# One decoder layer on one core: an opening with fewer waits, and a third expert pair returned to tokens by one-hot products

## The chip, the cores and the metric

The kernel runs on one core of a Trainium2 chip. The metric is the device time of one execution in microseconds. TensorE multiplies matrices into the eight banks of PSUM; VectorE (DVE), ScalarE (ACT) and GpSimd (POOL) work elementwise; SyncE (SP) and the others issue DMAs, which 16 DMA engines carry out.

## The reference

One layer of a decoder on x (512 tokens, 1024 channels), in float32:

```python
mod = silu(c) @ w_ada + b_ada                      # six vectors: shift, scale, gate, twice
h = rmsnorm(x, norm1) * (1 + sc1) + sh1
z = h @ w_in                                       # q, k, v, pooling input, two gates
merged = sigmoid(ga) * attention_branch + sigmoid(gp) * pooling_branch
x = x + g1 * (merged @ w_out)
h = rmsnorm(x, norm2) * (1 + sc2) + sh2
# router: best of 4 groups, then the best 2 of its 8 experts; weights e_w
for each of 32 experts e:
    hid = silu(h @ w1[e]) * (h @ w3[e]) * combine[:, e]      # 256 hidden channels
    out = out + hid @ w2[e]
x = x + g2 * out
```

w_ada is 24 MB, w_in 16 MB, and each expert has 3 MB of weights (w1, w3 and w2 of 1 MB each), 96 MB in all.

## The kernel before, in words

**Opening.** SP loads c, then the chunks of w_ada, x and w_in one behind the other, on one queue. TensorE forms the first two vectors of `mod` as rows (`ada_rows`) and turns them into columns (`ada_columns`), and transposes the normed x (`x_transposes`). Before the transposes it waits in program order for eight small vectors (`small_loaded`), since one small product (`vecs`, line 778) stands there. `keep_warm` is a helper that issues products nobody reads. The first unit of the w_in projection (line 638) then needs the columns of `mod`, hT, which ScalarE and VectorE make from them, and the first chunk of w_in.

**Middle.** 32 units of 128 output columns or rows with the attention, pooling and merging beside them, then `project`, the residual, the second norm and the router. SP starts on expert weights as arena space comes free.

**Routing.** VectorE copies the router's logits out of PSUM (line 1544) and picks experts; TensorE ranks the tokens; `one_hot` writes a matrix of tokens by slots for the pairs of experts in three groups (pairs 0 and 1, 2 and 3, 4 to 15). A pair is two experts of 64 slots each. `slot_sums` (line 887) multiplies these by token numbers (`tokb`, N = 2) and by the second choice (`oh2b`, N = 2) in products of their own; `indices` makes from them the rows to gather and to scatter. GpSimd gathers 128 rows of a pair from memory (line 1940).

**Pairs.** Step q runs `gate_up(q)` (w1 and w3, line 930), `gather_transposes(q + 1)`, `down(q - 1)` (w2, line 966), with tanh and copies on ScalarE and `modulate_gathered`, `hidden`, `drain_y` on VectorE, each in the order written. Six slots of weights form a ring, so three pairs are loaded ahead. SP waits until a pair's slots are free and issues the loads of the pair that follows; for experts 6 and 7 it does so by halves, the first half after four of the eight k of pair 0 (`ab_half`, lines 526 and on). The third group of slot sums stands inside `gate_up(1)`.

**End.** The results of pairs 0 to 13 go to `y_scratch` in memory by an indirect DMA (line 1945). When these have landed, SP loads them back by token, in four loads of 1 MB (`rows_of`, line 578), and VectorE adds the two rows of each token, weighted (`add_stored`, line 1690). Pairs 14 and 15 (`LAST = 2`) stay on the chip: `drain_last` (line 1673) weights them, ScalarE and VectorE split them into two parts (`y_high` line 1236, `y_low` line 1683), and TensorE multiplies by a one-hot matrix of slots and tokens (`spread`, line 983), two products for each of eight tiles and each pair. `down(15)` waits until `drain_last(0)` has emptied its PSUM banks. At last VectorE adds each of the eight tiles (line 1783) and SP stores it.

## Time and profile before

| | us |
|---|---|
| median of three runs | 651.97 (650.91 to 656.72) |
| the profiled execution's own time | 651.78 |
| its span, first to last instruction | 650.0 |
| TensorE busy | 579.4 (89%) |
| VectorE busy | 298.2 (46%) |
| ScalarE busy | 154.5 (24%) |
| DMA | 173.82 MB, mean 267 GB/s |

Busy time is a sum over stages with different limits, so it does not say which engine sets the time of a stage. The page's row by slices does: it has the DMA rate in each fortieth of the span. Mean granted clock of TensorE is 0.962 of full.

### The profile page before, as it was taken

To read this page: it belongs to the slowest core of one execution; us is meant where nothing else is said; L and a number is where in the kernel's file an instruction comes from. 1 tells how busy PE (TensorE), PEld (TensorE's weight loads), DVE (VectorE), ACT (ScalarE), POOL (GpSimd) and SP (SyncE) were. 2 spreads that over 40 slices of the span, in tenths; PEclk is the share of its full clock that TensorE was granted. 3 is DMA by queue.
4 is the path that set the end of the run, shared out by engine and by line. 5 is a ranking of instruction groups with operands and counts; after the bars stand their busy time and mean duration, and the time that the engine had idled before them with its cause. 6 is when DMAs were issued, how large, how long until landed. Compare 5 with 4: busy or idle time off the path is not lost.

```text
span 650.0 us, 7287 instructions
## 1 busy us (share of the span) xinstructions
PE 579.4 (89%) x2780; PEld 334.3 (51%) x2780; DVE 298.2 (46%) x580; ACT 154.5 (24%) x336; POOL 96.0 (15%) x144
## 2 busy tenths in 40 slices
PE   2699899999999999999999998999977888797891
PEld 0454577777766676764588844433322333232341
DVE  0227977455746565129624486323222222245258
ACT  3016013244433434333202302112111111111110
POOL 3022233059400000000000011111111111101000
PEclk9689899999999999999999989999998889898997
DMA  8994763403490606051457595899999999999873
GB/s 312 398 355 175 270 248 140 152 1 130 163 354 22 238 1 259 2 204 55 177 234 300 183 421 163 319 417 420 419 420 421 418 422 420 420 419 420 373 301 131
DMA packets 42073, 173.82 MB, mean 267 GB/s; under 512 B 6333, under 2 KB 6397, under 8 KB 29749
## 3 DMA queue, kind: packets, MB, share of 16 engines
q1 hardware_dynamic: 34704, 159.40, 61.9%
q0 software_dynamic: 5744, 12.84, 5.4%
q10 hardware_dynamic: 1588, 1.10, 0.5%
q8 instruction: 23, 0.38, 0.2%
q14 instruction: 14, 0.11, 0.0%
HBM read 165.36 MB, written 15.74 MB: 279 GB/s over the span
## 4 chain that ended last, share of the span: by engine, by line
PE 67%; DMA 10%; issue 8%; DVE 6%; SPq 4%; POOL 3%; ACTq 1%; ACT 0%; DVEq 0%; POOLq 0%
PE bank L930 15%; PE bank L966 7%; PE bank L649 5%; PE bank L651 5%; PE bank L650 5%; PE bank L739 4%; DMA late<-in_w_dram 4%; SPq L518 3%; POOL ss L1909 3%; DMA late<-in_w_in_dram 3%; DMA qkg<-in_k_norm_dram 2%; PE bank L831 2%; PE bank L833 2%; PE bank L832 2%; PE bank L913 2%
## 5 line engine op out<-in xcount | busy, mean ns | idle before, releaser
L930 PE MATMUL bank<-arena,hT 128*64 128x512 f32 x352 | 86.3, 633 | 16.9 <-issue 16.8
L649 PE MATMUL bank<-hT_high,w_in_parts 128*128 128x512 f32 x160 | 66.2, 414 | 0.0
L1649 DVE SCALAR_TENSOR_TENSOR g1b<-g1b,bank 128x256 f32<-128x256 f32 x16 | 6.7, 420 | 124.2 <-ACT g1b L1215 124.2
L651 PE MATMUL bank<-hT_high,w_in_parts 128*128 128x512 f32 x160 | 62.7, 392 | 0.0
L650 PE MATMUL bank<-hT_low,w_in_parts 128*128 128x512 f32 x160 | 62.4, 390 | 0.0
L930 PEld LDWEIGHTS bank<-arena,hT 128*64 128x64 f32 x352 | 26.2, 145 | 65.5 <-issue 64.1
L930 PE MATMUL bank<-late,hT 128*64 128x512 f32 x160 | 39.4, 638 | 9.5 <-issue 5.6
L966 PE MATMUL bank<-arena,g1b 128*64 128x512 f32 x176 | 40.2, 598 | 1.2 <-DVE acc L1673 1.2
L1221 ACT COPY g1b<-bank 128x256 f32<-128x256 f32 x16 | 6.0, 372 | 131.0 <-PE bank L948 131.0
L1940 POOL DMA_INDIRECT hT<-xn_scratch,gidx x16 | 16.4, 1028 | 139.2 <-PE bank L913 121.8
L1391 DVE TENSOR_REDUCE st<-bank 128x2 f32<-128x256 f32 (+3 forms) x16 | 13.2, 823 | 45.2 <-PE bank L675 45.2
L651 PEld LDWEIGHTS bank<-hT_high,w_in_parts 128*128 128x128 f32 x160 | 30.0, 188 | 6.6
L650 PEld LDWEIGHTS bank<-hT_low,w_in_parts 128*128 128x128 f32 x160 | 30.2, 189 | 5.8 <-issue 0.5
L649 PEld LDWEIGHTS bank<-hT_high,w_in_parts 128*128 128x128 f32 x160 | 30.1, 188 | 5.7 <-issue 0.6
L1207 ACT ACTIVATE hT<-bank,ab 128x128 f32<-128x128 f32 x64 | 24.0, 456 | 26.5 <-PE bank L913 26.5
L638 PE MATMUL bank<-arena,hT 128*128 128x512 f32 x64 | 29.7, 623 | 0.3 <-DVE hT L1344 0.3
L642 PE MATMUL bank<-w_in_chunk_high,hT_high 128*128 128x512 f32 x64 | 27.0, 422 | 2.6 <-issue 2.6
L930 PEld LDWEIGHTS bank<-late,hT 128*64 128x64 f32 x160 | 12.2, 146 | 32.6 <-issue 32.0
L739 PE MATMUL bank<-arena 128*128 128x512 f32 x64 | 27.6, 592 | 0.0
L644 PE MATMUL bank<-w_in_chunk_high,hT_low 128*128 128x512 f32 x64 | 25.7, 402 | 0.0
L643 PE MATMUL bank<-w_in_chunk_low,hT_high 128*128 128x512 f32 x64 | 25.5, 398 | 0.0
L1909 POOL TENSOR_TENSOR ss<-ss,nhalf 128x8 f32<-128x8 f32 x8 | 17.9, 2231 | 49.9 <-DVE ss L1368 49.9
(291 smaller groups left out, 963.8 us busy)
## 6 DMA issues: line engine op xcount, KB each, us to landing
arena<-in_w_dram SPq DMA_DIRECT2D x62, 1024.0 KB, 25.7
late<-in_w_dram SPq DMA_DIRECT2D x30, 1024.0 KB, 27.1
late<-in_w_ada_dram SPq DMA_DIRECT2D x6, 2048.0 KB, 12.7
arena<-in_w_ada_dram SPq DMA_DIRECT2D x5, 2048.0 KB, 9.1
arena<-in_w_in_dram SPq DMA_DIRECT2D x4, 2048.0 KB, 10.7
late<-in_w_in_dram SPq DMA_DIRECT2D x4, 2048.0 KB, 15.8
y_scratch<-arena POOLq DMA_DIRECT2D x1, 4096.0 KB, 17.8
late<-in_w_out_dram SPq DMA_DIRECT2D x2, 2048.0 KB, 7.9
```

Source lines behind the costliest of these rows:

```text
L638: last = mm(bank[:, u % 2, :], hT[:, k, m:m + P], w[:, k, :], start=k == 0, stop=k == 7)
L642: mm(bank[:, u % 2, :], hH[:, k, m:m + P], cH[:, k, :], start=k == 0, stop=False)
L643: mm(bank[:, u % 2, :], hH[:, k, m:m + P], cL[:, k, :], start=False, stop=False)
L644: last = mm(bank[:, u % 2, :], hL[:, k, m:m + P], cH[:, k, :], start=False, stop=k == 7)
L649: mm(bank[:, b, :], wH[:, b, k, :], hH[:, k, :], start=k == 0, stop=False)
L650: mm(bank[:, b, :], wH[:, b, k, :], hL[:, k, :], start=False, stop=False)
L651: last = mm(bank[:, b, :], wL[:, b, k, :], hH[:, k, :], start=False, stop=k == 7)
L739: last = mm(bank[:, b, :], wu[:, kk, P * m:P * (m + 1)], attnT[:, kk, :], start=kk == 0, stop=kk == HP - 1)
L930: last = mm(bank[SLOTS * x:SLOTS * (x + 1), 2 + q % 2, :].rearrange("p (w f) -> p w f", w=2), xgT[q % 2][:, k, SLOTS * x:SLOTS * (x + 1)], ...
L966: last = mm(bank[SLOTS * x:SLOTS * (x + 1), 6 + h, :], hidT[:, q % 2, ft, SLOTS * x:SLOTS * (x + 1)], w2s[s][:, ft, CH * h:CH * (h + 1)], ...
L1207: last = sc.activation(xgT[q % 2][:, k, :], bank[:, 1, P * (k % 4):P * (k % 4 + 1)], ACT.Identity, bias=ab2[:, 1, k:k + 1], scale=ab2[:, 0 ...
L1909: g.tensor_tensor(ss[:, u % 2, 1, :], ss[:, u % 2, 0, :], nhalf[:, :], ALU.pow).then_inc(qk_rstd, 1)
```

## The change

Four things change.

1. In the opening the wait for the small vectors and their product come after the transposes; 16 filler products stand in front of the transposes, 3 more behind `ada_rows(1, 1)`.
2. In the routing the logits are read where they lie in PSUM; the two right-hand sides of the slot sums are put side by side in one tile `sums`, so that one product with N = 4 takes the place of two with N = 2. VectorE writes this tile with two copies, where it wrote one.
3. Pair 0 waits for its input k by k. The loads of experts 8 and 9 go by halves as well, so their first half is issued half a projection earlier.
4. `LAST = 3`: pairs 13, 14 and 15 go through `spread`, pairs 0 to 12 through memory. The buffers `yg` and `yHL` are laid out anew, and SP waits for `ab_done` of 14 pairs before it loads the rows back. In step 15 VectorE now runs, in this order: `y_low(0)`, `hidden(15)`, `add_stored(0)`, `drain_last(1)`, `y_low(1)`; TensorE runs two tiles of `spread` ahead of `down(15)` and the others behind it.

```diff
@@ -46,7 +46,7 @@
 OUT_OF_BOUNDS = 4096
-LAST = 2
+LAST = 3
 STORED = PAIRS - LAST
...
@@ -217,14 +217,15 @@
-        yg = carve(AR, 12288, TT, 2, D)
-        yHL = nc.alloc_sbuf_tensor_at("y_parts", [P, LAST, 2, D], F32R, offset=arena_at + 4 * 20480)
-        spreadT = nc.alloc_sbuf_tensor_at("slot_to_token", [P, LAST, TT, P], F32R, offset=hT_at + 4 * 1024)
+        yg = [carve(AR, a, 2, D) for a in (12288, 14336, 18432, 20480)]
+        yHL = [nc.alloc_sbuf_tensor_at(f"y_parts_{i}", [P, 2, D], F32R, offset=a)
+               for i, a in enumerate((arena_at + 4 * 16384, arena_at + 4 * 22528, late_at))]
+        spreadT = nc.alloc_sbuf_tensor_at("slot_to_token", [P, LAST, TT, P], F32R, offset=hT_at + 4 * 512)
         iota_t = HT[:, 0:T]
 ...
         cws, toks = sm[:, 0:LAST], sm[:, LAST:2 * LAST]
-        cwe, cwr = (sm[:, a:a + TT * 2 * LAST].rearrange("p (t e) -> p t e", t=TT) for a in (4, 20))
-        cparts = sm[:, 36:60].bitcast(BF16).rearrange("p (t e c) -> p t e c", t=TT, c=3)
+        cwe, cwr = (sm[:, a:a + TT * 2 * LAST].rearrange("p (t e) -> p t e", t=TT) for a in (6, 30))
+        cparts = sm[:, 54:90].bitcast(BF16).rearrange("p (t e c) -> p t e c", t=TT, c=3)
...
@@ -241,11 +242,13 @@
         work = worker(RT, 2 * D)
-        lg = work(TT, NG + E)
         geq, goh, gdif, gexp, gpen = (work(TT, NG) for _ in range(5))
 ...
         em, eq1, maskf, rm = (work(TT, E) for _ in range(4))
-        maskm, oh2b = (work(TT * E // 2).bitcast(BF16).rearrange("p (t e) -> p t e", t=TT) for _ in range(2))
+        maskm = work(TT * E // 2).bitcast(BF16).rearrange("p (t e) -> p t e", t=TT)
+
+
+        sums = work(TT * PAIRS * 2).bitcast(BF16).rearrange("p (t q c) -> p t q c", t=TT, q=PAIRS)
         tokg = work(PAIRS)
...
@@ -524,7 +527,7 @@
                     sp.dma_start(dst, src[e][:, n * half:n * (half + 1)]).then_inc(
-                        w13_loaded[s] if half else w13_first, 16)
+                        w13_loaded[s] if half else w13_first[s // 2], 16)
...
@@ -535,6 +538,9 @@
                         load13(e + j, (e + j) % RING)
+                load2_pair(e)
+
+            def load2_pair(e):
                 sp.wait_ge(y_done, e // 2 + 1 - RING // 2)
...
@@ -557,11 +563,13 @@
             load2(5, 5)
-            for half in range(2):
-                sp.wait_ge(*((ab_done, 1) if half else (ab_half, 1)))
-                for j in range(2):
-                    load13_half(RING + j, j, half)
-            for e in range(RING, E, 2):
+            for q in range(2):
+                for half in range(2):
+                    sp.wait_ge(*((ab_done, q + 1) if half else (ab_half, q + 1)))
+                    for s in (2 * q, 2 * q + 1):
+                        load13_half(RING + s, s, half)
+            load2_pair(RING)
+            for e in range(RING + 2, E, 2):
                 load_pair(e)
...
@@ -774,17 +783,19 @@
             pe.wait_ge(consts_ready, 1)
-            pe.wait_ge(small_loaded, 16 * SMALL)
-            mm(bank[:, 6, 16:48], vecs, ident[0:32, 0:32], start=True, stop=True).then_inc(vecs_ready, 1)
+            keep_warm(16, 6, P, P)
             for t in range(TT):
 ...
                 x_transposes(range(6), t)
+            pe.wait_ge(small_loaded, 16 * SMALL)
+            mm(bank[:, 6, 16:48], vecs, ident[0:32, 0:32], start=True, stop=True).then_inc(vecs_ready, 1)
             ada_rows(0, 1)
 ...
             ada_rows(1, 1)
+            keep_warm(3, 6, P, P)
             ada_columns(1)
...
@@ -880,12 +891,11 @@
-                    for c, rhs in ((0, tokb[:, :, :]), (2, oh2b[:, :, 2 * q:2 * q + 2])):
-                        for t in range(TT):
-                            e = 2 * (q - IDX_GROUPS[g][0])
-                            lhs = place[g][t][:, e:e + 2, :].rearrange("p e s -> p (e s)")
-                            last = mm(idx_bank(g)[:, 4 * q + c:4 * q + c + 2], lhs, rhs[:, t, :],
-                                      start=t == 0, stop=t == TT - 1)
+                    for t in range(TT):
+                        e = 2 * (q - IDX_GROUPS[g][0])
+                        lhs = place[g][t][:, e:e + 2, :].rearrange("p e s -> p (e s)")
+                        last = mm(idx_bank(g)[:, 4 * q:4 * q + 4], lhs, sums[:, t, q, :],
+                                  start=t == 0, stop=t == TT - 1)
                     if q >= STORED:
...
@@ -903,11 +913,13 @@
+            X0 = KT // 2 - 1
+
             def gather_transposes(q):
 ...
                 if q >= 1:
-                    pe.wait_ge(xgT_ready, q)
+                    pe.wait_ge(xgT_ready, X0 + q)
                     pe.wait_ge(xgT_act, q)
...
@@ -917,21 +929,27 @@
                 slots = [(2 * q + x) % RING for x in range(2)]
-                if q == RING // 2:
-                    pe.wait_ge(w13_first, 64)
+                if q in (RING // 2, RING // 2 + 1):
+                    pe.wait_ge(w13_first[q - RING // 2], 64)
                 for s in slots:
                     pe.wait_ge(w13_loaded[s], 32 * (2 * q // RING + 1))
-                pe.wait_ge(xgT_ready, q + 1)
-                pe.wait_ge(xgT_act, q + 1)
+                if q >= 1:
+                    pe.wait_ge(xgT_ready, X0 + q + 1)
+                    pe.wait_ge(xgT_act, q + 1)
                 if q >= 2:
 ...
                 for k in range(KT):
+                    if q == 0 and k < KT // 2:
+                        pe.wait_ge(xgT_ready, k + 1)
+                    if q == 0 and k == KT // 2:
+                        pe.wait_ge(xgT_act, 1)
                     for x, s in enumerate(slots):
 ...
                                   start=k == 0, stop=k == KT - 1)
+                    if q < 2 and k == KT // 2 - 1:
+                        last.then_inc(ab_half, 1)
                     if q == 0 and k == KT // 2 - 1:
-                        last.then_inc(ab_half, 1)
                         gather_transposes(1)
...
@@ -992,15 +1010,21 @@
             hidden_transposes(PAIRS - 1)
-            down(PAIRS - 1)
             pe.wait_ge(spreadT_ready, 1)
             pe.wait_ge(yL_ready, 1)
+            for n in range(2):
+                spread(STORED, n)
+            down(PAIRS - 1)
+            for n in range(2, 6):
+                spread(STORED, n)
+            pe.wait_ge(yL_ready, 2)
             for n in range(6):
-                spread(STORED, n)
+                spread(STORED + 1, n)
             for h in range(2):
                 pe.wait_ge(y_last, h + 1)
-                spread(STORED, 6 + h)
-                pe.wait_ge(yL_ready, 2 + h)
+                for q in range(STORED, PAIRS - 1):
+                    spread(q, 6 + h)
+                pe.wait_ge(yL_ready, LAST + h)
                 for n in range(TT * h, TT * (h + 1)):
...
@@ -1226,21 +1250,24 @@
                     hidden_copy(q - 1)
+                if q == PAIRS - 1:
+                    for h in range(2):
+                        y_high(0, h)
                 hidden_tanh(q)
 ...
                 w = slice(CH * h, CH * (h + 1))
-                act.wait_ge(*((y_drained, STORED + 1) if i == 0 else (y_last, h + 1)))
-                sc.copy(yHL[:, i, 0, w], ysb[(STORED + i) % 3][:, w]).then_inc(yH_ready, 1)
+                act.wait_ge(*((y_drained, STORED + i + 1) if i < LAST - 1 else (y_last, h + 1)))
+                sc.copy(yHL[i][:, 0, w], ysb[(STORED + i) % 3][:, w]).then_inc(yH_ready, 1)
 ...
                 for h in range(2):
-                    y_high(0, h)
+                    y_high(1, h)
...
@@ -1541,7 +1568,7 @@
             S4, S32 = [P, TT, NG], [P, TT, E]
-            link(v.tensor_copy(lg, bank[:, 6, 0:TT * 36].rearrange("p (t n) -> p t n", t=TT)))
+            lg = bank[:, 6, 0:TT * 36].rearrange("p (t n) -> p t n", t=TT)
             gl, el = lg[:, :, 0:NG], lg[:, :, NG:NG + E]
...
@@ -1567,7 +1594,8 @@
             v.tensor_tensor(edif, best2, best1, ALU.subtract).then_inc(exp_in, 1)
-            v.tensor_copy(oh2b, oh2)
+            v.tensor_copy(sums[:, :, :, 2:4], oh2.rearrange("p t (q x) -> p t q x", x=2))
+            v.tensor_copy(sums[:, :, :, 0:2], tokb[:, :, :].unsqueeze(2).broadcast_to([P, TT, PAIRS, 2]))
             link(v.tensor_tensor(maskf, oh1, oh2, ALU.add))
...
@@ -1640,7 +1668,8 @@
                                            ab2[:, 0, k:k + 1], ab2[:, 1, k:k + 1], ALU.mult, ALU.add)
-                last.then_inc(xgT_ready, 1)
+                    if q == 0 or k == KT // 2 - 1:
+                        last.then_inc(xgT_ready, 1)
...
@@ -1672,22 +1701,23 @@
                                                   in1=g2b[:, w], op0=ALU.mult, op1=ALU.mult)
-                    if i == 1:
+                    if i == LAST - 1:
                         last.then_inc(y_last, 1)
-                if i == 0:
+                if i < LAST - 1:
                     last.then_inc(y_drained, 1)
 ...
                 dve.wait_ge(yH_ready, 2 * i + h + 1)
-                last = v.tensor_tensor(yHL[:, i, 1, w], ysb[(STORED + i) % 3][:, w], yHL[:, i, 0, w].bitcast(F32),
+                last = v.tensor_tensor(yHL[i][:, 1, w], ysb[(STORED + i) % 3][:, w], yHL[i][:, 0, w].bitcast(F32),
                                        ALU.subtract)
-                if i == 1 or h == 1:
+                if i == LAST - 1 or h == 1:
                     last.then_inc(yL_ready, 1)
-            def add_stored(t):
+            def add_stored(t, done=None):
+                dve.wait_ge(*(done or (yg_loaded[t], 16)))
                 for j in range(2):
-                    last = v.scalar_tensor_tensor(out=xs[:, t, :], in0=yg[:, t, j, :], scalar=cw[:, j, t:t + 1],
+                    last = v.scalar_tensor_tensor(out=xs[:, t, :], in0=yg[t][:, j, :], scalar=cw[:, j, t:t + 1],
                                                   in1=xs[:, t, :], op0=ALU.mult, op1=ALU.add)
...
@@ -1706,14 +1736,21 @@
                     weights_by_slot()
-                hidden(q)
                 if q == PAIRS - 1:
-                    drain_last(0)
                     for h in range(2):
                         y_low(0, h)
+                hidden(q)
                 if 1 <= q < PAIRS - 1:
                     modulate_gathered(q + 1)
+                if 1 <= q <= STORED:
                     drain_y(q - 1)
+                elif q == STORED + 1:
+                    drain_last(0)
+                elif q == PAIRS - 1:
+                    add_stored(0)
+                    drain_last(1)
+                    for h in range(2):
+                        y_low(1, h)
...
@@ -1771,13 +1808,12 @@
             for h in range(2):
-                drain_last(1, range(h, h + 1))
+                drain_last(LAST - 1, range(h, h + 1))
             for h in range(2):
-                y_low(1, h)
+                y_low(LAST - 1, h)
             for n in range(2 * TT):
                 t, w = n % TT, slice(CH * (n // TT), CH * (n // TT + 1))
-                if n < TT:
-                    dve.wait_ge(yg_loaded[t], 16)
+                if 1 <= n < TT:
                     add_stored(t)
```

## Rows read from the trace of the kernel before

**Rows 1.** the page's 40 slices of 16.25 us each: GB/s moved by the DMA engines

```profile
GB/s 312 398 355 175 270 248 140 152 1 130 163 354 22 238 1 259 2 204 55 177 234 300 183 421 163 319 417 420 419 420 421 418 422 420 420 419 420 373 301 131
```

**Rows 2.** timeline of the opening: start, us, engine, line, operation, idle before

```profile
10.46 3.45 PE L755 MATMUL bank<-arena,probs 128*32 128x512 f32 x16 [10.46 <-DMA arena<-in_w_ada_dram]
...
18.37 2.74 DVE L1313 TENSOR_SCALAR late<-xs,st 128x1024 f32<-128x1024 f32 x4 [1.17 <-POOL st L1897]
...
20.98 0.60 PE L778 MATMUL bank<-ident,probs 32*128 32x32 f32 x2 [7.07 <-DMA qkg<-in_k_norm_dram]
...
21.51 5.38 PE L615 MATMUL bank<-ident,late 128*128 128x128 f32 x24
...
32.66 2.95 PE L771 MATMUL bank<-ones,ident 128*128 128x128 f32 x24
...
37.66 1.14 POOL L1899 DMA_DIRECT2D cols<-in_pool_scale_dram  x1 [19.33 <-DMA arena<-in_w_in_dram]
```

**Rows 3.** the chain of waits at the first projection unit, timeline at the third

```profile
40.52 8.82 PE bank L638 x16
...
56.46 7.03 PE L638 MATMUL bank<-arena,hT 128*128 128x512 f32 x16
```

**Rows 4.** timeline of VectorE and GpSimd in the routing

```profile
374.57 0.31 DVE L1544 COPY acc<-bank 128x144 f32<-128x144 f32 x1 [2.92 <-PE bank L852]
...
385.08 1.32 POOL L1940 DMA_INDIRECT hT<-xn_scratch,gidx  x1 [17.10 <-DVE gidx L1594]
```

**Rows 5.** gathers from xn_scratch issued at 380:392 and at 392:398, issue to landing

```profile
DMA to landing us min/median/max: 5.8/6.0/6.3
...
DMA to landing us min/median/max: 3.6/3.6/3.6
```

**Rows 6.** timeline of TensorE before the first expert pair

```profile
392.50 1.88 PE L771 MATMUL bank<-g2b,ident 128*128 128x512 f32 x4
```

**Rows 7.** windows of 2 us after the first expert pair; the last two columns are DMA share and GB/s

```profile
412.00:414.00 2.00, 2.00 (x11) 0.51 (x7) 0.00 (x0) 0.00 (x0) 0.00 (x0) 1.00 0.09 33
414.00:416.00 2.00, 2.00 (x14) 1.31 (x16) 1.51 (x5) 1.26 (x4) 0.09 (x1) 1.00 0.39 82
```

**Rows 8.** the chain of waits in the second pair's projection

```profile
404.02 0.95 PE bank L887 x32
...
409.97 0.44 PE bank L948 x2
```

**Rows 9.** timeline of SP's and GpSimd's DMA issues at the end

```profile
593.29 4.31 SPq L530 DMA_DIRECT2D arena<-in_w_dram  x2
...
595.39 1.00 POOL L1945 DMA_INDIRECT y_scratch<-probs,sidx  x1 [3.89 <-DVE probs L1661]
...
621.32 2.08 SPq L578 DMA_DIRECT2D arena<-y_scratch  x4
```

**Rows 10.** landing of the first load of 593.29, of that scatter, of the four row loads

```profile
arena<-in_w_dram SPq DMA_DIRECT2D x1, 1024.0 KB, 28.2
...
y_scratch<-probs,sidx POOLq DMA_INDIRECT x1, 7.9
...
DMA to landing us min/median/max: 5.2/8.3/11.3
```

**Rows 11.** timeline of TensorE and VectorE in the end

```profile
624.24 1.41 DVE L1673 SCALAR_TENSOR_TENSOR acc<-bank,ones,g2b 128x512 f32<-128x512 f32 x2 [2.22 <-PE bank L966]
...
625.80 3.65 PE L966 MATMUL bank<-arena,g1b 128*64 128x512 f32 x16 [1.25 <-DVE acc L1673]
...
629.38 7.55 PE L983 MATMUL bank<-y_parts,slot_to_token 128*128 128x512 f32 x32
...
631.60 2.60 DVE L1690 SCALAR_TENSOR_TENSOR xs<-arena,cw,xs 128x1024 f32<-128x1024 f32 x2
...
643.95 3.08 DVE L1783 TENSOR_TENSOR xs<-bank,xs 128x512 f32<-128x512 f32 x5
```

**Rows 12.** timeline of TensorE: a gate projection after a wait for weights

```profile
499.01 4.97 PE L930 MATMUL bank<-late,hT 128*64 128x512 f32 x16 [3.84 <-issue]
```

More of the change, by code:

```diff
@@ L364, in hybrid_trunk @@
         w13_loaded = [sem(f"w13_loaded{i}") for i in range(RING)]
-        w13_first = sem("w13_first")
+        w13_first = [sem(f"w13_first{i}") for i in range(2)]
         w2_loaded = [sem(f"w2_loaded{i}") for i in range(RING)]
@@ L982, in spread @@
                 for part in range(2):
-                    last = mm(bank[:, n, :], spreadT[:, i, t, :], yHL[:, i, part, w],
+                    last = mm(bank[:, n, :], spreadT[:, i, t, :], yHL[i][:, part, w],
                               start=i == 0 and part == 0, stop=i == LAST - 1 and part == 1)
@@ L1250, in _ @@
             for h in range(2):
-                y_high(1, h)
+                y_high(LAST - 1, h)
             def overflow(b):
```

8 lines of the change are left out of this document (4 added, 4 removed).

## The prediction

> **What bounds the kernel now.** I read the page's row by slices first. From the slice at 430 us to the one at 600 us the DMA engines move about 420 GB/s without a pause, and nowhere before for so long [rows 1]. So there are two regimes: up to about 400 us a chain of compute sets the time, and the weights are a side stream; from about 415 us on the stream of expert weights sets it, and TensorE waits. Then I read the chain of waits, which agrees: units of TensorE up to 480 us, then weights, and in the end VectorE. Last I read the timelines of the four places that the change touches. The question for each gain is how it gets into the stream, and for each cost whether it stands behind the stream's end. Times of the end below are of the old kernel's clock; the sum subtracts what the stream gains.
>
> **The opening.** TensorE goes idle at 13.91 us, waits for the small vectors until 20.98, then transposes from 21.51 to 26.89 [rows 2]. The first tile of x is normed at about 19.1 and the last at 21.1, the end of the four operations begun at 18.37. With the wait moved back and the array kept busy, the 24 transposes are paced by VectorE and end near 21.9: six behind the last tile at 2.95/24 = 0.12 us. The 16 fillers are 32 instructions (12 gave 24): 3.9 us at that price, 7.2 at the 5.38/24 = 0.22 us of the transposes, thus done between 17.8 and 21.1, no later than the last tile. The columns would be done some 4.9 us earlier. But the first unit also needs its chunk of w_in, which landed at 37.66, when GpSimd, which waits for that chunk alone, went on [rows 2]. The queue is busy throughout, so nothing lands earlier. The unit began at 40.52 [rows 3]; it can begin at 37.7. I take 2.8 us. Below, the gain is 0, if the fillers end late and the transposes then run at the slow price. Above, it is 4.6: the first unit's 16 products took 8.82 us where the third's took 7.03 [rows 3], and if the fillers spare it that, 1.8 us is added; I give nothing, because in the new order TensorE idles between 36 and 37.7 just before. The 3 fillers behind ada_rows (0.7 us by the price above) lie beside VectorE's copy of the row. Without that cover they would cost 0.7. What follows is chained to the first unit, DMAs included, so it all moves by 2.8 us.
>
> **Routing.** The copy of the logits goes: 0.31 us [rows 4]. In group 0 8 of 16 slot products go, at 0.95/32 = 0.03 us each [rows 8]: 0.2. The added copy that widens the token numbers (at most the 0.31 us of the copy that goes) lies beside TensorE's ranking; uncovered it would cost just what is saved. So the first gather is issued 0.5 us earlier. It was issued at 385.08 and took 6.3 us beside the preload of weights; the gather of 393.49, with that done, took 3.6 [rows 4, 5]. So part of its time is the preload's. Bounds 0 and 0.5; I take 0.2. The Trainium skill, "DMA: Bandwidth & Descriptors", Queues, rings and completion order, says that each DMA engine takes turns, packet by packet, between the queues that have work; by this the gather does not stand behind the preload, its 0.5 us comes through in full, and the sum would be 0.3 us lower.
>
> **Pair 0 k by k: nothing.** The filler products before gate_up(0) run from 392.50 to 394.38 [rows 6], and the eight pieces of input are there by then. If they were not, the fine waits could give 1 us at most.
>
> **The gap in the stream.** The preload is over at 391, and loads start again only as slots come free. Of the 4 us from 412 to 416 the DMA engines are busy 0.09 x 2 + 0.39 x 2 = 1.0 us [rows 7]: the loads of experts 6 and 7 are over at 412.2, and those of 8 and 9 begin to move only at 415.2, behind the end of gate_up(1). The change issues half of them at the fourth k of that projection, 409.97 [rows 8], and that point itself comes 1.2 us earlier, since 44 net slot products go (48 fewer, 4 more for pair 13) at 0.03 us. The queue then has 2 MB more at about 409 to 410 and does not run dry. From here on everything waits for this queue, so the gap is a gain in full: 3.0 us. Bounds 1.1 (only the shift of the slot products, if another gap opens later) and 3.3. I see no such gap: a pair asks for 6 MB, and 6.3 MB at 0.42 MB/us is 15 us, against TensorE's 12.
>
> **Sum into the stream:** 2.8 + 0.2 + 3.0 = 6.0 us earlier for the last weights.
>
> **The end.** Pair 13 no longer goes through memory. Its scatter was the last thing that SP waited for before it issued the row loads at 621.32; now the last scatter is that of 595.39, landed 7.9 us later, at 603.3 [rows 9, 10]. So the row loads are issued 18 us earlier. But they stand on the same queue behind the w2 loads of experts 30 and 31, issued from 593.29 on, the first of which takes 28.2 us, to 621.5 [rows 9, 10], and the second follows at about 624. The first row load landed 5.2 us after its issue, at 626.5, and the last 11.3 after, at 633.9 [rows 10]. I take this order to hold, and take off 0.5 us for the missing scatter of 0.26 MB: first rows at 626.0.
>
> This matters because of the order on VectorE. In step 15 add_stored(0) stands in front of drain_last(1), and down(15) waits for drain_last(1). Before, VectorE went idle 2.22 us, drained from 624.24, and down(15) ran from 625.80 [rows 11]. Now it waits for the rows until 626.0, adds for 2.6, drains for 1.4, and down(15) starts at about 630.2: **4.4 us later.** Queued behind that wait are the drain, y_low of pair 14, and all that follows down(15). If the rows were there by 622, the add would take idle time and delay the drain by 0.4 only. TensorE covers 1 us of this with four spread products, then idles 4.7 us. After an idle 3.84 us the next 16 products took 4.97 instead of the 3.65 of an undisturbed group [rows 11, 12]; other waits of the trace cost up to 2. I add 1.5 (0 to 2.3).
>
> Spreads: 48 products instead of 32, at 7.55/32 = 0.236 us [rows 11]. Before the first tile is done, 26 now stand behind down(15), where 16 did: 6.1 us. VectorE's first add began at 634.2, 4.8 behind the end of down(15) at 629.4, because add_stored(0) stood there until then [rows 11]. So the third pair costs 1.3 us, and what add_stored(0) frees is not a gain: from the first tile on, the chain is the same three row adds and eight tiles, 634.2 to 647.0. Without spreads in the way it would have freed up to 2.5. Further adds on VectorE (0.43 for a third one-hot matrix, two y_low of 0.7) lie in its idle time before 621.
>
> End: 4.4 + 1.5 + 1.3 = 7.2 us later.
>
> **The sum:** 651.78 (span 650.0 and 1.8 around it) - 6.0 + 7.2 = 653.0. The execution profiled lies 0.2 under the median, so against the runs I expect 653.2; I write 653.0. What a measurement of this kernel can tell from no change is about 1%, 6.5 us; this is no change.
>
> **Rivals.**
> 1. *The row loads overtake.* The DMA engines do not all end together: the rate falls in the last slices [rows 1], so early issue could fill idle engines and bring the first rows by 622. Then the end costs 0.4 + 1.3: 651.78 - 6.0 + 1.7 = 647.5. Against it: a load has landed only when its last part has, and w2 itself landed until 624. With the first unit spared its slow start as well, 645.7. Chance 0.28.
> 2. *The opening gives nothing,* the fillers ending late: 655.8. Chance 0.12.
> 3. *Slower.* The four row loads share the engines, so the first lands with the last, at 633.9: add_stored(0) holds drain_last(1) until 636.5, down(15) starts at 638.1, 12.3 us late; 651.78 - 6.0 + 12.3 + 1.5 + 1.3 = 660.9. It passes 1% once the first rows land later than about 631. Against it: before, the landings were spread from 5.2 to 11.3 us, one behind the other. Chance 0.09.
> 4. *The stream has another gap* and the ring gives 1.1: 654.9. Chance 0.06.
>
> My forecast has the remaining 0.45. The range is 645.5 to 658: it takes in rivals 1, 2 and 4 and the clock's and the gather's bounds, and leaves out most of rival 3. Faster by over 1% needs rival 1 and a better opening or routing: 0.13. Slower by over 1%: rival 3 or rival 2 with the clock's full price: 0.08. Within 1%: 0.79.
>
> **What would show it.** Opening: the first unit at 37.7 us. Gap: no slice under 300 GB/s between 410 and 420. Stream: w2 of expert 31 landed near 618, 6 us earlier. End: add_stored(0) waiting for a row load and released some 4 us after hidden(15); drain_last(1) right behind it; down(15) starting near 624.2, its first products slow; first tile added 6 us behind the end of down(15). The forecast is wrong if VectorE finds the rows there, or if the first unit does not start earlier.

## The result, and the profile after

The changed kernel takes 655.08 us (median of 20 runs), the kernel before 651.71 in the same comparison; run against run the ratio is **1.0038, interval 1.002 to 1.0057**, 2.5 us slower (the ratio leaves out one execution of 659.96 us, which was in a slower state). That is under 1% and so "no change" by the bound set above, but it is a real loss, and, as the experiments below show, two large parts stand behind it: the front of the kernel became about 5 us faster, the end about 7 us slower.

Each later ratio is to the kernel before, with a 95% interval, and one hundredth of it is 6.5 us. A profile is one execution, and the profiled starts of the same unit differ by 3 us and more between kernels whose code up to there is the same; the sections below therefore take durations inside a stage from the profiles and the worth of a part from the ratios.

**The opening.** Timeline of TensorE in the changed kernel (start, us, engine, line, operation, idle before), answering to [rows 2, 3]:

```profile
14.10 3.91 PE L780 MATMUL bank<-ones,ident 128*128 128x128 f32 x32
19.39 2.86 PE L624 MATMUL bank<-ident,late 128*128 128x128 f32 x24 [1.38 <-DVE late L1340]
...
27.23 3.00 PE L764 MATMUL bank<-late,probs 128*32 128x512 f32 x16 [0.85 <-DMA late<-in_w_ada_dram]
...
38.58 13.97 PE L647 MATMUL bank<-arena,hT 128*128 128x512 f32 x32 [0.27 <-DVE hT L1371]
```

The 16 fillers take 3.91 us, the transposes 2.86 instead of 5.38 and start 2.1 earlier. The 4.6 us by which the transposes end earlier (22.25 against 26.89) do not arrive whole: at 27.23 TensorE meets the second weight chunk of the conditioning, which had just landed, and its products take 3.00 us where they took 1.92 before. The first unit starts at 38.58, not at 40.52, and takes about 7, not 8.82.

**The routing and the first pair,** the same view, answering to [rows 4, 6], GpSimd's issue first:

```profile
381.00 1.32 POOL L1975 DMA_INDIRECT hT<-xn_scratch,gidx  x1 [16.56 <-DVE gidx L1622]
...
388.34 1.14 PE L925 MATMUL bank<-ident,hT 128*128 128x128 f32 x8 [2.35 <-DMA hT<-xn_scratch,gidx]
389.31 3.18 PE L780 MATMUL bank<-g2b,ident 128*128 128x512 f32 x4
392.43 4.00 PE L947 MATMUL bank<-arena,hT 128*64 128x512 f32 x16
```

and of the kernel before:

```profile
391.55 1.12 PE L913 MATMUL bank<-ident,hT 128*128 128x128 f32 x8 [1.27 <-DMA hT<-xn_scratch,gidx]
...
394.41 3.65 PE L930 MATMUL bank<-arena,hT 128*64 128x512 f32 x16
```

The gather is issued 4.1 us earlier, TensorE's transposes start 3.2 earlier, gate_up(0) only 2.0 earlier: the four fillers behind the gather took 3.18 us instead of the 1.88 of [rows 6].

**The stream behind the second pair,** windows of 2 us (last columns: DMA share, GB/s), answering to [rows 7]:

```profile
404.00:406.00 2.00, 2.00 (x45) 1.17 (x44) 0.00 (x0) 0.00 (x0) 0.00 (x0) 1.00 1.00 342
406.00:408.00 2.00, 2.00 (x18) 0.84 (x16) 1.58 (x10) 0.29 (x1) 0.00 (x0) 1.00 1.02 416
...
412.00:414.00 2.00, 2.00 (x12) 0.77 (x12) 1.84 (x6) 1.50 (x4) 0.83 (x1) 1.00 0.98 303
414.00:416.00 2.00, 2.00 (x12) 0.72 (x10) 0.03 (x1) 0.00 (x0) 0.16 (x1) 1.00 0.96 268
```

The gap (shares 0.09 and 0.39) is closed. But the queue, now always busy, moves 303 and 268 GB/s in these two windows and not 420.

**The end.** Timeline of SP, TensorE and VectorE, answering to [rows 9, 11]:

```profile
601.96 2.46 SPq L586 DMA_DIRECT2D arena<-y_scratch  x4
...
609.19 6.54 PE L947 MATMUL bank<-arena,hT 128*64 128x512 f32 x16 [4.04 <-issue]
...
621.49 2.60 DVE L1720 SCALAR_TENSOR_TENSOR xs<-arena,cw,xs 128x1024 f32<-128x1024 f32 x2 [0.40 <-DMA arena<-y_scratch]
624.13 1.41 DVE L1702 SCALAR_TENSOR_TENSOR acc<-bank,ones,g2b 128x512 f32<-128x512 f32 x2
...
625.68 3.65 PE L984 MATMUL bank<-arena,g1b 128*64 128x512 f32 x16 [1.14 <-DVE acc L1702]
...
635.54 0.69 DVE L1819 TENSOR_TENSOR xs<-bank,xs 128x512 f32<-128x512 f32 x1 [3.96 <-PE bank L1001]
...
645.25 3.08 DVE L1819 TENSOR_TENSOR xs<-bank,xs 128x512 f32<-128x512 f32 x5
```

and the landing of the four row loads (issue to landing), answering to the last of [rows 10]:

```profile
DMA to landing us min/median/max: 19.5/22.6/25.6
```

Here is the reading that misleads. The row loads are issued 19.4 us earlier than at [rows 9] and the first lands at 601.96 + 19.5 = 621.5, 5 us earlier than before: they stand behind the weights. add_stored(0) waited only 0.40 us for it. But the last gate projection, gate_up(15), took 6.54 us where it took 3.65 before, at a granted clock of 0.50, so hidden(15) came 2.9 us late, and so most of the wait for the rows was spent as slow products ahead of it. One profile could not say which of the two costs the time. The experiments could.

### The profile page after: what moved, and what is told of

Same layout as the page of the kernel before. It is cut to its first block, busy times and chain, and to the rows that moved or that the text cites. A ratio compares the mean times of both kernels' runs of the same rounds, so it can differ in the third digit from the quotient of the medians.

```text
span 651.3 us, 7283 instructions
## 1 busy us (share of the span) xinstructions
PE 585.2 (90%) x2774; PEld 337.4 (52%) x2774; DVE 300.5 (46%) x585; ACT 155.7 (24%) x338; POOL 95.0 (15%) x143
## 4 chain that ended last, share of the span: by engine, by line
PE 68%; DMA 11%; issue 9%; DVE 7%; POOL 3%; SPq 1%; ACT 0%; ACTq 0%; DVEq 0%; POOLq 0%
PE bank L947 16%; PE bank L984 8%; PE bank L658 5%; PE bank L660 5%; PE bank L659 5%; PE bank L748 4%; DMA late<-in_w_ada_dram 3%; DMA arena<-y_scratch 3%; DMA late<-in_w_in_dram 3%; POOL ss L1944 3%; PE bank L925 3%; PE bank L842 2%; PE bank L843 2%; PE bank L844 2%; DVE xs L1720 2%
## 5 line engine op out<-in xcount | busy, mean ns | idle before, releaser
L947 PE MATMUL bank<-late,hT 128*64 128x512 f32 x160 | 40.8, 657 | 10.0 <-issue 10.0
L647 PE MATMUL bank<-arena,hT 128*128 128x512 f32 x64 | 28.0, 593 | 0.3 <-DVE hT L1371 0.3
L652 PE MATMUL bank<-w_in_chunk_low,hT_high 128*128 128x512 f32 x64 | 25.6, 400 | 0.0
L843 PE MATMUL bank<-w_out_low,merged_high 128*128 128x512 f32 x64 | 24.9, 389 | 0.0
```

The lines of the kernel that those rows point to most:

```text
L647: last = mm(bank[:, u % 2, :], hT[:, k, m:m + P], w[:, k, :], start=k == 0, stop=k == 7)
L652: mm(bank[:, u % 2, :], hH[:, k, m:m + P], cL[:, k, :], start=False, stop=False)
L843: mm(bank[:, n % 2, :], mH[:, k, ts], oL[:, h, k, :], start=False, stop=False)
L947: last = mm(bank[SLOTS * x:SLOTS * (x + 1), 2 + q % 2, :].rearrange("p (w f) -> p w f", w=2), xgT[q % 2][:, k, SLOTS * x:SLOTS * (x + 1)], ...
```

## The experiments

Three places were in question: what the end costs and by which wait, whether the stream's gain is whole, and whether routing helps. The first four kernels split the change.

**Everything but the end.**

```
 the changed kernel:
-LAST = 3
+LAST = 2          (and the code of the end as before)
```

> The whole change but its fourth part: LAST stays 2 and the end is the old one. Theory A (terms add as predicted: opening 2.8, routing 0.2, gap 3.0): 6.0 us faster than before, 645.8, ratio 0.991. Theory B (read from the changed kernel's trace: the last gate projection began only 3.8 us earlier, then ran 2.9 us slow after a wait of 4.0 us): the stream gives 3.8 us, and 0 to 2.9 of it go to the slow start, so 1 to 4 us faster, ratio 0.994 to 0.999.

Measured 0.9922 (0.9891 to 0.9953): 5.1 us faster than before. Against the changed kernel's 1.0038 the end costs 7.6 us, with some 2.3 either way by the two intervals.

**The end alone.**

```
 the kernel before:
-LAST = 2
+LAST = 3          (and all that follows from it at the end)
```

> The old kernel with the fourth part alone (LAST = 3, rows issued early, add_stored(0) ahead of drain_last(1)). Theory A (the drain waits for the rows, 4.4, TensorE starts slow, 1.5, spreads 1.3): 7.2 us slower, 659, ratio 1.011. Theory B (rows come 0.8 us late as in the changed kernel, whatever the last projections do, and spreads cost 1.3): 2.1 us slower, ratio 1.003. The profile decides: the wait of add_stored(0) for a row load is about 3.5 to 4 us by A, under 1 by B.

Measured 1.0072 (1.0049 to 1.0094): 4.7 us slower. This lies between the two theories, and in its profile too the last gate projection is slow (6.55 us) and add_stored(0) waits only 0.37. It is also 2.9 us less than the 7.6 above, about as much as the intervals of the two allow.

**The opening alone.**

```
 the kernel before:
-            pe.wait_ge(small_loaded, 16 * SMALL)
-            mm(bank[:, 6, 16:48], vecs, ident[0:32, 0:32], ...)
+            keep_warm(16, 6, P, P)
...
+            keep_warm(3, 6, P, P)
```

> The old kernel with the new opening alone. Theory A: the first unit begins at 37.7 us and all follows 2.8 us earlier, to the end: ratio 0.996. Theory B (changed kernel's trace: first unit 1.9 us earlier and 1.7 us shorter): 3.6 us earlier, ratio 0.9945. Theory C: the gain is there at 360 us but is lost where TensorE's clock falls in the routing: 1 to 2 us, ratio 0.998.

Measured 0.9957 (0.9931 to 0.9983): 2.8 us faster; first unit at 38.52.

**The loads of experts 8 and 9 in halves, and pair 0 k by k.**

```
 the kernel before:
-            for half in range(2):
-                sp.wait_ge(*((ab_done, 1) if half else (ab_half, 1)))
+            for q in range(2):
+                for half in range(2):
+                    sp.wait_ge(*((ab_done, q + 1) if half else (ab_half, q + 1)))
```

> The old kernel with the loads of experts 8 and 9 by halves and pair 0 k by k. Theory A: the gap of 3 us in the DMA stream closes and the end comes 3.0 us earlier, ratio 0.995. Theory B: the gap closes but half loads move slower (the changed kernel's windows of 412 to 416 us show a DMA share of 0.97 at 285 GB/s, against 420 elsewhere), so 1.5 us, ratio 0.9975. In the profile: windows of 412 to 416 us with a share near 1 and under 320 GB/s by B, at about 420 by A.

Measured 0.9953 (0.9923 to 0.9983): 3.1 us faster. This kernel has the old opening, and yet its first unit looks like this (timeline of TensorE), against 40.52 and 8.82 for 16 products in [rows 3]:

```profile
39.27 10.97 PE L643 MATMUL bank<-arena,hT 128*128 128x512 f32 x25 [0.27 <-DVE hT L1357]
```

So the old opening has two outcomes: in the profiles of three kernels with it the first unit began at 39.3 to 39.8 and took 7.12 us, in two, the profile that the prediction was made from among them, at 40.5 to 40.6 and took 8.82. Against the first kind the new opening saves about 1 us, against the second about 3.7 (first unit over at 45.6 in the opening alone, at 46.4 to 46.9 and at 49.3 and 49.5 with the old one).

**The stored rows added where they were before.** This takes away the one wait that the prediction blamed, and leaves all else of the change:

```
 the changed kernel, VectorE:
                 elif q == PAIRS - 1:
-                    add_stored(0)
                     drain_last(1)
...
-                if 1 <= n < TT:
+                if n < TT:
                     add_stored(t)
```

> The changed kernel, but add_stored(0) back at its old place, behind y_low of the last pair, so that drain_last(1) and down(15) do not wait for a row load. VectorE sits idle there for 4.0 us in the changed kernel's trace, so the 2.6 us of the add are free. Theory A (the order costs what I predicted, 4.4 and up to 1.5 for the clock, in executions where the last gate projection is not slow): 1 to 4 us faster than the changed kernel, so 0.994 to 1.000 of the old one. Theory B (the order costs the 0.8 us of the profiled execution): 1.003. Theory C (the order costs nothing; rows are there): 1.004, as the changed kernel.

Measured 0.9934 (0.9909 to 0.9958): 6.8 us faster than the changed kernel (some 2 either way), and not to be told from the kernel without the end. The place of that one addition costs more than the whole loss. Its end (TensorE and VectorE):

```profile
608.56 3.65 PE L947 MATMUL bank<-arena,hT 128*64 128x512 f32 x16 [1.95 <-issue]
...
621.36 3.65 PE L984 MATMUL bank<-arena,g1b 128*64 128x512 f32 x16 [0.32 <-DVE acc L1702]
...
627.17 2.60 DVE L1720 SCALAR_TENSOR_TENSOR xs<-arena,cw,xs 128x1024 f32<-128x1024 f32 x2
...
640.96 3.08 DVE L1818 TENSOR_TENSOR xs<-bank,xs 128x512 f32<-128x512 f32 x5
```

**The changed kernel again.** A second execution's profile, to see the wait without the slow projection before it. No edit.

> The changed kernel once more, nothing altered: a second profiled execution and a second ratio. Ratio expected 1.002 to 1.006. Theory A (the sum of the last pair waits for the row loads, and in the first profiled execution that wait was hidden behind a last gate projection that itself ran 6.54 us on a slow TensorE): wherever the last gate projection takes about 3.65 us, add_stored(0) waits 3 to 4 us for the rows, which land about 12.3 us behind the projection's start; where it takes 6.5, the wait is 0.4. Theory B (the rows are in time, and the end costs something else): the wait is under 1 us whatever the projection takes.

Measured 1.0043 (1.0022 to 1.0065), the same loss. Timeline of TensorE and VectorE at the end:

```profile
608.63 3.65 PE L947 MATMUL bank<-arena,hT 128*64 128x512 f32 x16 [1.77 <-issue]
...
620.91 2.60 DVE L1720 SCALAR_TENSOR_TENSOR xs<-arena,cw,xs 128x1024 f32<-128x1024 f32 x2 [3.27 <-DMA arena<-y_scratch]
623.55 1.41 DVE L1702 SCALAR_TENSOR_TENSOR acc<-bank,ones,g2b 128x512 f32<-128x512 f32 x2
...
625.11 5.00 PE L984 MATMUL bank<-arena,g1b 128*64 128x512 f32 x16 [4.00 <-DVE acc L1702]
630.03 10.27 PE L1001 MATMUL bank<-y_parts,slot_to_token 128*128 128x512 f32 x44
...
645.98 3.08 DVE L1819 TENSOR_TENSOR xs<-bank,xs 128x512 f32<-128x512 f32 x5
```

Its chain of waits (start, us, what):

```profile
591.09 8.13 DMA y_scratch<-probs,sidx
599.24 21.65 DMA arena<-y_scratch
620.91 1.30 DVE xs L1720
622.23 1.30 DVE xs L1720
623.55 1.42 DVE acc L1702 x2
625.11 5.00 PE bank L984 x16
```

With gate_up(15) at 3.65 us the wait is open to see: 3.27 us for the rows, TensorE idle 4.00, and down(15) slow behind it, 5.00 instead of 3.65. The rows are there 620.91 - 608.63 = 12.3 us after the start of the gate projection; in the first profile 621.49 - 609.19 = 12.3, in the kernel with the end alone 622.08 - 609.79 = 12.3. In the kernel with the rows added late, where nobody waits for them, they land at 598.88 + 22.0, again 12.3 behind 608.56. They are tied to the stream, not to VectorE or to the moment of their issue. The expectation said so before the run.

**The end in all fourteen profiles.** From the start of gate_up(15) to the end of the last tile (for the kernel before 643.95 + 3.08 by [rows 11], less the start of that projection at 613.00, which took 3.65):

| end | kernels | gate_up(15), us | length of the end, us |
|---|---|---|---|
| two pairs | before, opening, halves, both with fillers before the last projection | 3.65 | 34.0 |
| two pairs | without the end | 4.99 | 35.4 |
| two pairs | whole loads, routing, opening with halves | 5.35 | 35.7 |
| three, rows added late | stored rows late | 3.65 | 35.5 |
| three, rows added late | the same with a filler | 5.11 | 36.9 |
| three, rows added early | the changed kernel, second profile | 3.65 | 40.4 |
| three, rows added early | the changed kernel, first profile; end alone | 6.54; 6.55 | 39.1 |

Where down(15) does not wait for rows, the length is a constant plus what the slow projection adds (34.0 + 1.34 = 35.4, 34.0 + 1.70 = 35.7). With the early add a slow projection adds nothing: the rows come when they come, and down(15) is spared its own slow start. The table gives each term: the third pair 35.5 - 34.0 = 1.5, the early add 40.4 - 35.5 = 4.9, in all 6.4.

**Fillers before the last gate projection.** Is its slow start worth curing?

```
 the kernel without the end, TensorE:
             counts.append(overflow_count(pe))
+            keep_warm(7, 5)
```

> The change without its fourth part (as e1), and 7 filler products (3.3 us) ahead of the last gate projection, where TensorE waits for the last w1 and w3. Theory A (the clock falls in that wait and costs 1.3 to 2.9 us on the path): 1.3 to 2.9 us faster than e1, ratio to the old kernel 0.988 to 0.990. Theory B (the row of the slow projection is not on the path, or the wait is mostly short): the same as e1, 0.992, or slower by up to 1 us where the fillers end after the weights have landed.

Measured 0.9992 (0.9966 to 1.0017): slower, not faster, than without. The 14 products took 6.28 us and ended at 613.5; one filler of two products costs 0.9 us, and I had sized it at half. So the dose was too large and the run told nothing on the idea. Three instead of seven:

```
+            keep_warm(3, 5)
```

> Everything changed but the end, and six filler products (some 2.7 us) ahead of the last gate projection, so that TensorE stands idle about 1.3 us instead of 4 before it. Theory A (the clock's fall in that idle time costs 1.3 to 2.9 us on the path that sets the end): 0.988 to 0.990, with the last gate projection at about 3.65 us. Theory B (the slow projection is covered by the wait for the last expert's other weights): same as without the fillers, 0.992, or slightly slower.

Measured 0.9954 (0.9931 to 0.9976). Timeline of TensorE:

```profile
604.87 2.84 PE L778 MATMUL bank<-g2b,ident 128*128 128x512 f32 x6
...
607.64 3.65 PE L945 MATMUL bank<-arena,hT 128*64 128x512 f32 x16
```

beside the kernel without the fillers:

```profile
612.66 4.99 PE L945 MATMUL bank<-arena,hT 128*64 128x512 f32 x16 [3.94 <-issue]
```

The projection is quick and the end has its short length (34.0 us in the table), as Theory A says; the ratio is not the 0.988 to 0.990 that it asks for. In the profile the projection starts with no idle time behind the fillers, so they may have held it up by part of what they save. Theory A falls as far as time goes: nothing is gained.

**Whole loads.** Are the loads in halves slow by themselves?

```
 the kernel before, SP (experts 6 and 7):
-            for half in range(2):
-                sp.wait_ge(*((ab_done, 1) if half else (ab_half, 1)))
-                for j in range(2):
-                    load13_half(RING + j, j, half)
+            sp.wait_ge(ab_done, 1)
+            for j in range(2):
+                load13(RING + j, j)
```

> The old kernel with w1 and w3 of experts 6 and 7 loaded whole at the end of pair 0's projection, not by halves. It starts them 5 us later, so 3 to 5 us slower, ratio 1.006. What it is for: the DMA rate while they move. Theory A (half loads, with 4 KB a partition each, are slow): windows at about 420 GB/s. Theory B (a gather beside them is slow whatever the size): windows of 270 to 340 GB/s at a share near 1, as in the kernels with halves.

Measured 1.0015 (0.9983 to 1.0047), no gain and no loss, where a loss of 3 to 5 us was expected. Windows of this kernel, where whole loads move throughout:

```profile
406.00:408.00 2.00, 2.00 (x45) 1.19 (x44) 0.00 (x0) 0.00 (x0) 0.00 (x0) 1.00 1.00 422
408.00:410.00 2.00, 2.00 (x15) 0.76 (x14) 1.64 (x10) 0.37 (x1) 0.00 (x0) 1.00 1.03 422
...
416.00:418.00 2.00, 2.00 (x12) 0.66 (x10) 0.12 (x1) 0.00 (x0) 0.07 (x1) 1.00 1.04 438
418.00:420.00 2.00, 2.00 (x12) 0.72 (x10) 1.17 (x2) 0.00 (x0) 0.00 (x0) 1.00 0.98 414
```

and of the kernel before, with experts 6 and 7 in halves:

```profile
402.00:404.00 2.00, 1.59 (x8) 0.29 (x4) 2.00 (x3) 0.38 (x1) 0.00 (x0) 1.00 1.05 330
404.00:406.00 2.00, 1.98 (x39) 1.16 (x40) 0.71 (x2) 0.00 (x0) 0.00 (x0) 1.00 0.92 266
```

Whole loads are not slowed by a gather: in the kernel with whole loads one is in flight from 415.08 for 9.2 us, and beside it they move 438 and 414 GB/s, 369 at the lowest (422 to 424). The two windows of the kernel before, 330 and 266 GB/s, lie beside a gather as well, issued at 399.92, and so do most of the windows under 350 of the changed kernel (gathers from 398.28 for 8.1 us and from 413.17 for 8.3). So one could think that it takes halves and a gather together. The kernel with opening and halves (last of the experiments) shows that this is not it. Its gather of 396.06 landed after 8.2 us; the next, in the timeline of GpSimd:

```profile
413.58 0.99 POOL L1956 DMA_INDIRECT hT<-xn_scratch,gidx  x1 [16.53 <-PE bank L922]
```

and windows of 2 us before and behind this gather:

```profile
408.00:410.00 2.00, 2.00 (x10) 0.66 (x8) 0.00 (x0) 0.00 (x0) 0.00 (x0) 0.83 1.05 330
410.00:412.00 2.00, 2.00 (x11) 0.69 (x8) 0.00 (x0) 0.28 (x1) 0.00 (x0) 1.00 0.89 291
...
416.00:418.00 2.00, 2.00 (x12) 0.69 (x10) 1.29 (x2) 0.00 (x0) 0.00 (x0) 1.00 1.03 420
418.00:420.00 2.00, 2.00 (x12) 0.62 (x8) 0.00 (x0) 0.00 (x0) 1.03 (x1) 1.00 1.03 402
```

The halves are slow before that gather is issued, with none in flight, and the engines are back at full rate beside it (it lands 8.5 us after its issue). What goes with the low rates is **which halves move**. The loads go out in sets of four, 2.1 MB or 512 packets of 4 KB: first halves of experts 6 and 7, their second halves, first halves of 8 and 9, their second halves. Counted by packets, in the thirteen profiles that have halves (four of them only the first two sets), a packet of the first or third set took 195 to 221 ns in the mean, one of the second or fourth 159 to 175. In the nine with all four sets the first set took 7.6 to 7.8 us, the second 5.2 to 5.5. Theory A as I wrote it, halves slow in any case, is too wide, and Theory B, the gather, is wrong. No run loaded the second halves first, so this is seen, and not tested by a change of its own. The time came out the same as with whole loads; one reading, not tested either, is that what the first halves lose in rate they have ahead in start.

**Routing alone.**

```
 the kernel before:
-        link(v.tensor_copy(lg, bank[:, 6, 0:TT * 36]...))
+        lg = bank[:, 6, 0:TT * 36]...
...
-                    for c, rhs in ((0, tokb[:, :, :]), (2, oh2b[:, :, 2 * q:2 * q + 2])):
+                        last = mm(idx_bank(g)[:, 4 * q:4 * q + 4], lhs, sums[:, t, q, :], ...)
```

> The old kernel with the routing alone (no copy of the logits, one product with N = 4 for two with N = 2). Theory A: 0.2 us up to the first gather's landing, and the 1.1 us of slot products inside the second pair's projection bring the loads of experts 8 and 9 forward, since the gap in the stream is still there: 1.3 us, ratio 0.998. Theory B: only the 0.2 us: 1.000. Theory C: the two copies on VectorE cost what the one saved: 1.000 and no earlier gather.

Measured 0.9983 (0.9961 to 1.0006), not to be told from none. Its timeline of TensorE:

```profile
392.12 1.54 PE L914 MATMUL bank<-ident,hT 128*128 128x128 f32 x8 [2.45 <-DMA hT<-xn_scratch,gidx]
393.46 3.19 PE L773 MATMUL bank<-g2b,ident 128*128 128x512 f32 x4
```

The gather was issued at 384.68, 0.4 us earlier than at [rows 4]; the transposes began at 392.12, 0.6 later. TensorE, done sooner, stood idle 2.45 us instead of 1.27, and the products behind ran slow.

**One more filler before the gather's transposes,** to keep TensorE busy there:

```
 the kernel with the stored rows late, TensorE:
             slot_sums(1)
-            keep_warm(4, 5)
+            keep_warm(5, 5)
```

> The changed kernel with the stored rows added where they were before, and one more filler product group (0.92 us) before the transposes of the first pair's gathered rows, so that TensorE stands idle about 1.4 us ahead of them instead of 2.3. Theory A (the routing work ends earlier but its gather does not land earlier, so TensorE stands idle for longer and its clock falls; the fillers behind the gather take 3.3 us instead of 1.9): 1.3 us faster than the same kernel without the filler, ratio to before about 0.991, and those fillers take about 1.9 us. Theory B (the longer fillers are hidden behind the expert weights or come from something else): same as without, 0.993, or the fillers still take 3.2 us.

Measured 0.995 (0.9924 to 0.9976). Timeline:

```profile
387.03 1.12 PE L925 MATMUL bank<-ident,hT 128*128 128x128 f32 x8 [1.12 <-DMA hT<-xn_scratch,gidx]
387.99 1.88 PE L780 MATMUL bank<-g2b,ident 128*128 128x512 f32 x4
389.80 3.65 PE L947 MATMUL bank<-arena,hT 128*64 128x512 f32 x16
```

The mechanism is as expected, 1.88 us instead of 3.33; the time is not: it is the same as without.

**Opening and halves, no routing, old end.** The parts of the change as in the second and fourth edits above, together.

> Opening and the pair stream of the first pairs changed, routing sums and the end as before. Theory A (the routing part costs as much by the slow clock as it gives): as fast as the kernel with routing too (0.992) or faster, 0.990 to 0.992, and the fillers behind the first gather take 1.9 us. Theory B (the routing part gives its 0.2 to 1.3 us): slower than that kernel, about 0.994.

Measured 0.9913 (0.9881 to 0.9944), the fastest of all, with its fillers at 1.88 us; with routing too it was 0.9922. The difference is far inside the intervals. Either of the two, and the one with the rows added late (0.9934), beats the kernel before and the changed one; they are not to be told from one another.

## Why the prediction was right, and where its sizes were off

The forecast was 653.0, by its own steps -6.0 into the stream and +7.2 at the end; measured 655.08 by the median, or by the ratio 2.5 us slower than before where 1.2 was forecast. The case that happened is the one given 0.45: no change by the 1% bound, with both large parts where they were put.

**The opening, -2.8.** Alone it gives 2.8 us (1.1 to 4.5). The number is right, partly by luck. The first unit started 0.9 later than the 37.7 forecast. The sum had only the chunk of w_in as the next thing in line; GpSimd's wait for that ended at 38.04 this time, and the unit then still waited for hT. What the sum had at nothing are slow products ahead of it: the second weight chunk and the 24 fillers behind it took 6.2 to 6.5 us together in six of the nine profiles with the new opening, and the unit began at 38.1 to 38.6, waiting for hT. In the other three they took 4.9, and it began at 37.4 to 37.7, waiting for w_in, as forecast. In all nine the unit itself was quick (about 7 us), for which I had given nothing. The later start and the quicker unit pull against each other; that 2.8 comes out is luck to that extent. What I could not see in one profile is that the old opening itself varies by over 1 us.

**Routing, -0.2.** Bounds 0 to 0.5; alone -1.1, with an interval from -2.5 to +0.4, and with opening and halves present +0.6. Nothing can be read from that but "small". The mechanism was incomplete: what ends earlier ahead of a gather that does not land earlier turns into idle time, and of the seven profiles that carry the routing part with the old number of fillers before the gather, six show the next four products slow, 3.18 to 3.62 us; in the seventh (six fillers before the last projection), where the idle time was 2.10 us and not 2.31 to 3.20, and in all six without the routing part, they took 1.88. The Trainium skill's rule that each DMA engine takes turns between the queues ("DMA: Bandwidth & Descriptors", Queues, rings and completion order) would have passed the 0.5 us on in full. The routing kernel does not show it: issued 0.4 earlier, used 0.6 later. In the changed kernel 4.1 us of earlier issue gave 3.2 of earlier use: the gather took 7.2 us instead of 6.3, with more of the preload beside it. The rule may hold packet by packet, which these runs do not show; the latency of a gather still depends on the bulk queue: 3.4 us with nothing beside it (the one of 399.08 in the kernel with whole loads), 8.1 to 9.2 beside weights.

**Pair 0 k by k, nothing.** gate_up(0) waits for nothing but the fillers in the profiles, as said. It was not run by itself.

**The gap, -3.0.** Measured, with pair 0 k by k, -3.1 (-5.0 to -1.1). The sign of this step that I named, no slice under 300 GB/s between 410 and 420, failed in one window of the changed kernel (268). The bytes of the gap are not all won: while the first halves of experts 8 and 9 move, 303 and 268 GB/s are about two thirds of the 420 of a full stream. The working had these loads at 0.42 MB/us throughout. That the time still came out at 3 us lies within a wide interval and does not confirm the step's working.

**Into the stream, -6.0.** All but the end gave -5.1 (-7.1 to -3.1); opening with halves -5.7. In the two profiles of the changed kernel gate_up(15) started at 609.19 and 608.63, 3.8 and 4.4 earlier than before; but in the profile of the kernel without the end, whose code is the same up to there, at 612.66 (an execution of 652.76 us, where the median was 648.49), so such starts do not size it. By the ratios the sum was about 1 us too large, well inside the measurement. Of the 1.3 us between the forecast and the measured loss 0.9 would lie here and 0.4 at the end.

**The end, +7.2 = 4.4 + 1.5 + 1.3.** This is the part the forecast rested on, and the table above sizes it: the wait for the rows delays down(15) by (625.11 - 608.63) - (621.36 - 608.56) = 3.7 instead of 4.4, because the rows land 12.3 us behind the start of gate_up(15) and not the 13.0 (626.0 - 613.00) that I took; TensorE's slow products cost 5.00 - 3.65 = 1.35 instead of 1.5; the third pair's spreads 1.5 instead of 1.3. Sum 6.4 by the profiles with a quick projection, 7.6 (some 2.3 either way) by the ratios. Where gate_up(15) is slow (6.54), the changed end costs less: 39.1 against the 34.0 + 2.9 = 36.9 that two pairs would take with such a projection, an estimate by the rule above, so 2.2. This the forecast did not have, since gate_up(15) took 3.65 in the profile of before. It may be why "the end alone" cost 4.7 us and not 7; no run counts how many executions are of either kind. Of the signs that I named, the first tile was added 6.2 us behind the end of down(15), as forecast; down(15) started at 625.68 and 625.11, not near 624.2; and the sign of being wrong, that VectorE finds the rows there, was nearly met in the first profile (0.40 us of wait). The second shows the wait, 3.27 us.

**Rival 1** (the row loads overtake) did not happen: issued 19.4 us earlier, landed 5. **Rival 2** (the opening gives nothing) neither. **Rival 3** asked for the four loads to share the engines: they landed at 19.5, 22.6 and 25.6 us (first, median, last), one behind the other. **Rival 4** (another gap) did not appear as an idle queue, but as a slow one.

**What stays open.** Why the first halves of the weight matrices move slowly, and second halves and whole loads do not, is not known from these runs. Whether the falling clock before the last gate projection and behind the first gather costs anything in the mean is also open: in the profiles it costs 1.3 to 2.9 us where it happens, and the fillers that prevent it gained nothing in time.

## What to carry to other kernels

A load that is issued earlier on a full queue still lands behind what stands ahead of it there (issued 19.4 us earlier, landed 5). Work that waits for it should not be moved ahead of work that does not, or the queue's end becomes the engine's wait, and whoever stands behind that engine pays as well. When the profile shows a small wait right behind an unusually slow stretch, take a second execution before sizing the wait: the slow stretch may be hiding it. And measure the parts of a change by themselves, for a total near zero here was +7 and -5, and without the one misplaced addition the rest is worth keeping (0.9934).

## What the runs showed of the hardware that I had not expected

- Of loads of half a weight matrix (4 KB in each partition) a packet took 195 to 221 ns in the mean in first halves, 159 to 175 in second halves, at a DMA share of about 1. It was not the gather: with opening and halves, the engines moved 330 and 291 GB/s over first halves with no gather in flight, 420 and 402 over second halves beside one. Whole loads (8 KB in each partition) moved 369 to 438 GB/s beside a gather.
- A gather of 128 rows took 3.4 us from issue to landing with nothing beside it, 8.1 to 8.3 beside halves, 9.2 beside whole loads.
- After an idle time of 2.3 to 3.2 us, four filler products took 3.2 to 3.6 us at a granted clock of 0.50 (1.2 GHz of 2.4), after 0.67 to 2.10 us they took 1.88; before the last gate projection an idle time near 4 us went with 4.99 to 6.55 us for 16 products instead of 3.65, and in one kernel so did one of 1.97 (5.35).
- A float32 product of 128 by 512 used as a filler costs 0.45 us (6.28 us for 14), one of 128 by 128 0.12 us (2.94 for 24).
